# Last row of modulation sums taken from TensorE to VectorE in a diffusion-transformer layer, with one ScalarE step per inverse root and a new table of chain distances

## What is computed

```python
mod = (silu(c) @ w_mod + b_mod)              # c: 2048, w_mod: 2048 x 12288
sh1, sc1, g1, sh2, sc2, g2 = split(mod, 6)   # six rows of 2048
h  = rms_norm(x, mix_norm_pre) * (1 + sc1) + sh1
p  = h @ w_in                                # likewise for the context
o  = bidirectional chunked gated delta rule of q, k, v (8 heads, chunks of 128 tokens here)
mix = concat(rms_norm(o) * silu(z), silu(layer_norm(depthwise_conv31(glu(p)))))
x  = x + g1 * rms_norm(mix @ w_out, mix_norm_post)
hf = rms_norm(x, ffn_norm_pre) * (1 + sc2) + sh2
x  = x + g2 * rms_norm((silu(hf @ w_gate) * (hf @ w_up)) @ w_down, ffn_norm_post)
```

## Time and profile before

| | |
|---|---|
| median of 3 runs | 1611.73 us (1609.91 to 1611.95) |
| profiled execution, its own time | 1613.92 us |
| its span in the trace | 1612.2 us |
| PE busy | 1538.3 us (95%) |
| DVE busy | 1033.4 us (64%) |
| ACT busy | 739.2 us (46%) |
| POOL busy | 222.2 us (14%) |
| read from memory | 331.15 MB, 207 GB/s over the span |

### The profile page before, as it was taken

One profiled execution on the slowest core, in us unless ns is written; L12 is line 12 of the kernel. 1 busy time (PEld: TensorE's weight loads), 2 busy tenths in 40 slices (PEclk: granted clock), 3 DMA queues, 4 the chain that ended last, 5 costly groups with the idle time before them and its releaser, 6 DMA issues.

```text
span 1612.2 us, 25110 instructions
## 1 busy us (share of the span) xinstructions
PE 1538.3 (95%) x9297; PEld 1295.0 (80%) x9297; DVE 1033.4 (64%) x1435; ACT 739.2 (46%) x1042; POOL 222.2 (14%) x236
## 2 busy tenths in 40 slices
PE   3888999999999999999999999999999999999998
PEld 0557888898889888898877888888888888888786
DVE  1446899999997766665577544545454454777554
ACT  5535534443345745455357444444444443443332
POOL 2000223333242324244100000000000000000000
PEclk9998999999999999999999999999999999999999
DMA  9994566555655556564373766666666666998653
GB/s 351 382 397 116 167 199 196 190 190 183 208 179 176 171 171 209 170 196 132 118 261 117 212 194 186 192 185 192 184 193 192 187 190 191 339 321 319 222 187 136
DMA packets 190977, 334.58 MB, mean 208 GB/s; under 512 B 14706, under 2 KB 80354, under 8 KB 189985
## 3 DMA queue, kind: packets, MB, share of 16 engines
q1 hardware_dynamic: 190194, 330.89, 63.3%
q0 software_dynamic: 688, 2.39, 0.5%
HBM read 331.15 MB, written 2.10 MB: 207 GB/s over the span
## 4 chain that ended last, share of the span: by engine, by line
PE 82%; DVE 9%; DMA 2%; ACT 2%; SPq 2%; issue 2%; DVEq 0%; ACTq 0%
PE PS L1886 67%; DVE cacc L1752 3%; DMA first<-in_w_mod_dram 2%; DVE w_lo L1465 2%; PE PS L2107 2%; PE PS L2155 2%; PE PS L1892 2%; PE PS L2201 2%; SPq L756 2%; DVE sil L1586 1%; PE PS L2053 1%; PE PS L2097 1%; PE PS L1982 1%; DVE xyi L1645 1%; ACT L973 1%
## 5 line engine op out<-in xcount | busy, mean ns | idle before, releaser
L977 ACT ACTIVATE w_hi<-raw 128x1024 fp32r<-128x1024 f32 (+1 forms) x422 | 443.2, 1056 | 494.8 <-PE PS L1886 418.1
L1432 DVE TENSOR_TENSOR w_lo<-raw,w_hi 128x1024 fp32r<-128x1024 f32 x264 | 323.0, 1225 | 309.9 <-ACT w_hi L977 309.8
L1886 PE MATMUL PS<-w_hi,h_hi 128*128 128x512 f32 x704 | 275.2, 391 | 0.0
L1886 PE MATMUL PS<-w_hi,h_lo 128*128 128x512 f32 x704 | 274.3, 390 | 0.0
L1886 PE MATMUL PS<-w_lo,h_hi 128*128 128x512 f32 x704 | 274.1, 389 | 0.0
L1886 PE MATMUL PS<-h_hi,w_hi 128*128 128x256 f32 (+1 forms) x784 | 237.6, 303 | 0.0
L1465 DVE TENSOR_TENSOR w_lo<-raw,w_hi 128x1024 fp32r<-128x1024 f32 (+1 forms) x158 | 195.8, 1250 | 56.5 <-ACT w_hi L977 56.5
L1886 PE MATMUL PS<-h_hi,w_lo 128*128 128x256 f32 (+1 forms) x784 | 221.5, 283 | 0.0
L1886 PE MATMUL PS<-h_lo,w_hi 128*128 128x256 f32 (+1 forms) x784 | 221.4, 282 | 0.0
L1886 PEld LDWEIGHTS PS<-h_hi,w_hi 128*128 128x128 f32 (+1 forms) x784 | 148.3, 189 | 36.1 <-issue 32.0
L1886 PEld LDWEIGHTS PS<-w_hi,h_lo 128*128 128x128 f32 x704 | 132.3, 188 | 27.6
(11 more groups left out here) (323 smaller groups left out, 2338.4 us busy)
## 6 DMA issues: line engine op xcount, KB each, us to landing
raw<-in_w_in_dram SPq DMA_DIRECT2D x128, 512.0 KB, 3.8
raw<-in_w_mod_dram SPq DMA_DIRECT2D x96, 512.0 KB, 5.3
raw<-in_w_gate_dram SPq DMA_DIRECT2D x88, 512.0 KB, 3.6
raw<-in_w_up_dram SPq DMA_DIRECT2D x88, 512.0 KB, 3.6
raw<-in_w_down_dram SPq DMA_DIRECT2D x88, 512.0 KB, 4.6
first<-in_w_mod_dram SPq DMA_DIRECT2D x64, 512.0 KB, 9.3
raw<-in_w_out_dram SPq DMA_DIRECT2D x32, 512.0 KB, 4.3
gin<-in_w_mod_dram SPq DMA_DIRECT2D x32, 512.0 KB, 6.0
```

Of the source, the lines that this page charges most:

```text
L977: act.activation(out_ap, in_ap, ACT.Copy).then_inc(S[kind], 1)
L1432: dve.tensor_tensor(w_lo[:, slot, :], raw[:, (R0 + n) % RING, :], w_hi[:, slot, :].bitcast(F32), ALU.subtract).then_inc(S["lo"], 1)
L1886: ins = pe.matmul(out_ap, a[i], b[j], start=start and n == 0, stop=stop and n == 2, skip_group_check=grouped)
```

## The change

1. The list of groups on TensorE is cut to two (g1 and sh2), spread with the same density as before, so that they are done after two thirds of the stream. The third group, sc2, is summed on VectorE. It is cut into four quarters q of 512 columns (`NQ` = 4), each into eight steps `md (q, j)`. A step reads one ring buffer that holds two slices of 128 x 512; with the per-partition scalar silu(c) it does `mrw = raw * c` for the very first slice and `mrw = raw * c + mrw` for the others: two VectorE instructions on 512 columns a step, the second waiting for the first, and the next step waiting for this one. 32 steps, 64 instructions.
2. After the eighth step of a quarter, `mcol (2, q)` sums `mrw` over the partitions on TensorE with four matmuls, each with a block of 128 columns of `mrw` as weights and one column of ones moving, and `mcc (2, q)` adds the bias on VectorE (128 x 4). So there are four such pairs where there was one, and the ScalarE copy `mrc` of the third group is gone.
3. The steps start 4 slots (`md0`) after both the last `dw` and the second group's `mcc` are placed, and come every 6 slots (`md`). All of them are in the list before `s2`.
4. The two ScalarE steps of each inverse root become one step that issues both instructions, with a wait on a semaphore of ScalarE's own (`ch_act`) between them.
5. The table `AFTER` has new numbers. The reload of x for the FFN gets a step name of its own (`xin`) in the same place.

```diff
-AFTER = {"nr": [4, 4, 4, 7, 4, 4, 4, 2], "nr_last": [2, 17, 6, 9, 4, 5, 2, 7], ...
+AFTER = {"nr": [4, 4, 4, 7, 4, 4, 4, 0], "nr_last": [0, 19, 5, 9, 0, 9, 4, 7], ...
...
+         9], "gates": 15, "conv": 4, "rush": 1, "md": 6, "md0": 4, "vb1": [1, 2, 0, 2, 1, 3, 0, 5]}
...
-    mr = [(grp, j) for grp in range(MR) for j in range(KT)]
+    mr = [(grp, j) for grp in range(MR - 1) for j in range(KT)]
+    rows = [x for q in range(NQ) for x in [[("md", (q, j))] for j in range(KT // 2)] + [
+        [("mcol", (MR - 1, q)), ("mcc", (MR - 1, q))]]]
...
+        if row_slot[0] is None and ("dw", (NP - 1, NDW - 1)) in placed and ("mcc", (MR - 2,)) in plan:
+            row_slot[0] = slot[0] + AFTER["md0"]
+        if rows and row_slot[0] is not None and slot[0] >= row_slot[0]:
+            put(rows.pop(0))
+            row_slot[0] += AFTER["md"]
...
-            gates(MR * KT * done // total - (MR * KT - len(mr)))
+            gates((MR - 1) * KT * 3 * done // (2 * total) - ((MR - 1) * KT - len(mr)))
...
     assert not any(queue for _, queue in queues)
+    assert not rows
     plan.append(("s2", ()))
+    plan.append(("xin", ()))
...
+            if u[0] == "md":
+                _, q, j = u
+                col = (1 + MR) * D + 512 * q
+                return w_mod_v[:, 2 * j:2 * j + 2, col:col + 512]
...
+                            elif old[0] == "md":
+                                need(sp, "md", *old[1:])
...
-            def inverse_root(out_ap, log_ap):
+            n_chain = [0]
+
+            def inverse_root(out_ap, log_ap, in_ap, eps, scale):
 
                 using(EXP_LN)
+                n_chain[0] += 1
+                act.activation(log_ap, in_ap, ACT.Ln, bias=eps, scale=scale).then_inc(ch_act, 1)
+                act.wait_ge(ch_act, n_chain[0])
                 return act.activation(out_ap, log_ap, ACT.Exp, scale=-0.5)
...
                 elif kind == "s2":
-                    need(dve, "mcc", 2)
+                    need(dve, "mcc", MR - 1, NQ - 1)
...
+                elif kind == "md":
+                    q, j = key
+                    n = at_ring["md", q, j]
+                    dve.wait_ge(landed[n % RING], 16 * (n // RING + 1))
+                    if j == 0:
+                        need(dve, "mcol", *((MR - 1, q - 1) if q else (MR - 2,)))
+                    for i in range(2):
+                        part, col = raw[:, n % RING, 512 * i:512 * (i + 1)], csil[:, LAT, 2 * j + i:2 * j + i + 1]
+                        if j or i:
+                            ins = dve.scalar_tensor_tensor(out=mrw[:, :], in0=part, scalar=col, in1=mrw[:, :],
+                                                           op0=ALU.mult, op1=ALU.add)
+                        else:
+                            ins = dve.tensor_scalar(mrw[:, :], part, col, None, ALU.mult)
+                        if i == 0:
+                            step(ins)
+                    ins.then_inc(done, 1)
+                    if j < KT // 2 - 1:
+                        need(dve, "md", q, j)
...
+                elif kind == "mcol" and key[0] == MR - 1:
+                    grp, q = key
+                    need(pe, "md", q, KT // 2 - 1)
+                    b = aux(pe, kind, key)
+                    for n in range(4):
+                        ins = pe.matmul(PS[:, b, n:n + 1], mrw[:, P * n:P * (n + 1)], ones[:, 0:1], start=True, stop=True)
                     ins.then_inc(done, 1)
```

More of the change, by code:

```diff
@@ L236, in make_plan @@
     slot = [0, 0, 0]
+    row_slot = [None]
     def advance():
@@ L277, in gates @@
                 plan.append(("mrc", (grp,)))
+                if grp == MR - 2:
+                    plan.extend([("mcol", (grp,)), ("mcc", (grp,))])
         del mr[:n]
@@ L320, in make_plan @@
             gates(len(mr))
-            plan.extend([("mcol", (MR - 1,)), ("mcc", (MR - 1,))])
         rest = [c[0] for c in STREAM[n:]]
@@ L350, in make_plan @@
         unit(("wo", c, kg), QS, beside)
-    assert not late and not soon
+    assert not late and not soon and not mr
     until(("mix_lo", (NP - 1,)))
     assert not any(queue for _, queue in queues)
+    assert not rows
     plan.append(("s2", ()))
+    plan.append(("xin", ()))
     for n, (c, kg) in enumerate(WO_REST):
@@ L476, in layer @@
     SQUARED = {name: [step for step in PLAN if step[0] == name] for name in ("ysq", "psq")}
-    UNITS = [u for u in RINGED if u[0] != "mr"]
+    UNITS = [u for u in RINGED if u[0] not in ("mr", "md")]
     at_unit = {u: n for n, u in enumerate(UNITS)}
@@ L611, in sem @@
             return es.enter_context(nc.semaphore(name))
-        S = {kind: sem(f"s_{kind}") for kind in TOTALS if kind not in ("fh", "fl", "ft")}
+        S = {kind: sem(f"s_{kind}") for kind in TOTALS if kind not in ("fh", "fl", "ft", "xin")}
         S["fh"], S["fl"] = S["hi"], S["lo"]
@@ L1046, in _ @@
                     need(act, "cst")
-                    using(EXP_LN)
-                    act.activation(rtmp[:, col], sums[:, col], ACT.Ln, bias=cst[:, 0:1],
-                                   scale=1.0 / D).then_inc(S[kind], 1)
-                elif kind == "xrc":
-                    s, col = key[0], slice(2 * key[0], 2 * key[0] + 2)
-                    if s == FFN:
-                        col = slice(4 + key[1], 5 + key[1])
-                    need(act, "xrt", *key)
-                    inverse_root(rstd[:, col], rtmp[:, col]).then_inc(S[kind], 1)
-                elif kind == "nrc":
-                    need(act, "nrt", *key)
-                    a = 8 if key[1] == "k" else 12
-                    inverse_root(rstd[:, a:a + 4], rtmp[:, a:a + 4]).then_inc(S[kind], 1)
+                    inverse_root(rstd[:, col], rtmp[:, col], sums[:, col], cst[:, 0:1], 1.0 / D).then_inc(S[kind], 1)
+                elif kind == "nrc":
+                    s, what, p = key
+                    need(act, "nsq", *key)
+                    a = 8 if what == "k" else 12
+                    inverse_root(rstd[:, a:a + 4], rtmp[:, a:a + 4], sums[:, a:a + 4],
+                                 cst[:, 0:1] if what == "k" else cst[:, 1:2],
+                                 1.0 if what == "k" else float(P)).then_inc(S[kind], 1)
@@ L1066, in _ @@
+                    inverse_root(cx[:, 0, :], cx[:, 1, :], cx[:, 0, :], cst[:, 0:1], 1.0 / DC).then_inc(S[kind], 1)
                 elif kind == "yrc":
                     t, = key
-                    need(act, "yrt", t)
-                    inverse_root(rstd[:, 6 + t:7 + t], rtmp[:, 6 + t:7 + t]).then_inc(S[kind], 1)
+                    need(act, "ysm", t)
+                    inverse_root(rstd[:, 6 + t:7 + t], rtmp[:, 6 + t:7 + t], sums[:, 6 + t:7 + t], cst[:, 0:1],
+                                 1.0 / D).then_inc(S[kind], 1)
@@ L1773, in _ @@
                     dve.tensor_tensor(cacc[:, :, :], cacc[:, :, :], bc(cx[:, 0, :], 1, 8), ALU.mult).then_inc(done, 1)
+                elif kind == "md":
[16 more added lines that the diff above has]
+                        need(dve, "md", q, j)
+                elif kind == "mcc" and key[0] == MR - 1:
+                    grp, q = key
+                    need(dve, "mcol", *key)
+                    at = KT * grp + 4 * q
+                    dve.tensor_tensor(modc[:, at:at + 4], PS[:, BANK["mcol", key], 0:4],
+                                      vcol[:, VC_MR + at:VC_MR + at + 4], ALU.add).then_inc(done, 1)
                 elif kind == "mcc":
```

87 lines of the change are left out of this document (30 added, 57 removed), and 10 rows, old and new, of the table AFTER.

## The result

The changed kernel takes 1617.01 us (median of 22 runs, 1613.23 to 1620.17) where the kernel before takes 1611.74 (22 runs, 1609.63 to 1614.1): ratio 1.0032, 95% interval 1.0025 to 1.004. The forecast was 1598.3. The profiled execution of the changed kernel has 1615.24 us of its own, the one of the kernel before 1613.92: these two are 1.3 us apart and the medians 5.3, so what the traces show side by side is only a part of the loss. What the row itself costs is read further on, against a kernel without it.

The account below looks back on a forecast made before the run. Behind the taps TensorE sets the pace, with 100 us of idle VectorE beside it. -17.6 + 1.2 + 3 = -13.4 us, so 1611.73 becomes 1598.3 us; forecast 1593 to 1604 (0.60), range 1592 to 1608 (about 8 in 10).

Parts of the forecast that it names:

- What TensorE loses, 17.6 us: Sixteen modulation steps leave TensorE behind the taps, 1.10 us each: 17.6 us off (15.5 to 18.6).
- What TensorE gets, 0.6 us a column step: Four new column steps on TensorE, 2.4 us, less 1.2 for the old one: 1.2 us on (0 to 3.6).
- VectorE's 51 us: 64 new product-and-sums, 47.7 us plus 3.7 for GpSimd's interference; VectorE 81% busy from 540 to 800 us.
- The stall: TensorE waiting for VectorE in the solve, at `gh` to `z`: 3 us on (0 to 9).
- The second way: Stall estimated from TensorE's empty share against VectorE's busy share in two stretches: 1.1 points of 260 us, 2.9 us.
- the row with 0.91: Earlier trace's stretch of granted clock 0.91, where TensorE waited 2.04 us for a seed; priced 0 in the sum.
- The loads, the roots, the table: Buffers freed by VectorE (at most 2 us), joined root steps, new step distances (-4 to 2.6): 0 each.
- VectorE's queue gives half back: Rival: in-order waits on VectorE count double, leaving about -3 to -8 us: 1604 to 1609; chance 0.15.
- The solve's chain becomes the bound: Rival: from `xadd` to `z`, 21 levels each later by 1.6 us: up to +17 us, 1629; chance 0.07.
- Its point of decision: For the solve-chain rival: above a mean stall of 16.4/32 = 0.5 us a step the change loses.
- What would show it wrong: Stretch waits for `gh`, `pi`, `w_lo` over 12 us, load waits, clock below 0.97 in several slices, or unchanged output-projection start.

Follow-up runs that it names:

- no_row: Changed kernel without the third group's 32 steps, their loads and products; the four column steps kept without their wait for the products: 1600.88 us, ratio 0.9929.
- the fourth quarter alone: Changed kernel with the third group's steps, loads and waits left out for the first three quarters, only the last eight steps kept: 1601.29 us, ratio 0.9936.
- the second quarter alone: Changed kernel with only the third group's steps and loads from 610 to 685 us kept, the other three quarters left out: 1609.84 us, ratio 0.999.

## Why the prediction was wrong

- **What TensorE loses, 17.6 us.** Not measured by itself. no_row, with the steps gone and no product in their place, gains 1611.74 - 1600.88 = 10.9, where the forecast's own terms give -17.6 + 1.2 = -16.4.
- **What TensorE gets, 0.6 us a column step.** Too low by a misreading: the earlier trace rows count records, and a matmul of this form is two. "Four of them take 0.36 us" were two matmuls. A column step is eight records, 0.81 us to the next projection matmul (607.57 to 608.38) and 0.1 for that one's slower start: 4 x 0.9 - 1.2 = 2.4 us on, not 1.2. A record of one moving column takes 0.81/8 = 0.10 us, as one of 16 does. The Trainium skill (TensorEngine Tiling (Array Packing), Instruction Overhead) says that a matmul of one moving column has the latency of one with 60, and gives each an overhead of about 60 cycles. That few columns save nothing agrees with these rows; the 60 cycles, 0.025 us at 2.4 GHz by an estimate from that page's figure, do not, where the row has 0.10. Of the 5.5 us between 16.4 and 10.9 the columns are 1.2 and TensorE's waits 2.8 (8.3 for 5.5); 1.5 stay open. The two profiled executions are 13.0 us apart: 2.1 ahead of the layer norm, 13.1 from there to the output projection, and the output projection is 2.1 longer.
- **VectorE's 51 us.** Too low: the 64 products took 55.4 us, and VectorE is busy for 54.5 us more over the whole span. A product took 752 ns at the median and up to 1777, 898 in the mean of the 56 in the stretch, where the forecast had 802. That the stretch still has 211.25 us for the 211 of the forecast is luck: four products fell behind its end.
- **The stall: "I take 3 us on (0 to 9)". This is the step that failed;** measured 16.1. It was priced on one link, `gh` to `z`, with 3.7 us of slack in the mean. TensorE waits there 1.1 us in the changed kernel, 0.5 more than without the row. The row adds 8.7 us of waits, most of them elsewhere: 3.7 for the products' own column step, a wait that the change itself adds and that I had listed as 0.1 us of changeover; 2.4 for seeds and 1.2 for `xf_lat`, the longest of them directly behind products in VectorE's queue; and 1.1 through ScalarE, where `kd` holds up the copy of `pi` and `sil` the transposes. About 5.0 more come by the clock. The second way, from VectorE's share (61.5 to 81%), took a mean over stretches where the price is 0.4 us for one quarter and 9.0 for another with the same load. And no clock was in the price, though the row with 0.91 was there.
- **The loads, the roots, the table: 0 each.** Right: 0.8 us for the loads with a short product each, and ratios of 1.0002 and 1.0007 for roots and table, 1 inside both intervals. But the parts are not independent: with the products in, the old table costs 8 us.
- **The rivals.** "VectorE's queue gives half back" had the mechanism (in-order waits, the column sum, a late seed with a lower clock) at no more than 14.6 us with its columns and loads; the queue alone took 16.1. "The solve's chain becomes the bound" had the sign. Its point of decision, a mean stall of 0.51 us a step, fits by luck: 16.1/32 is 0.50, just below it, and the change loses because its gain without the row is 10.9 us and not 16.4. The way it went, every level late by a step, is not what the trace shows: the levels fall behind those of the kernel with the fourth quarter alone by 3 to 5 us at each of three places (590 to 630, 665 to 680 and 685 to 718 us) and keep step between them.
- **What would show it wrong** did: waits for `pi`, `gh` and `w_lo` stayed below the 12 us named (7.2 for `pi`, 1.1 for `gh`), but the clock was below 0.97 in three slices and the output projection started at the same time (756.6 us, before 757.6). That the FFN's length would stay the same was right.

## What to carry to other kernels

Before work is moved into an engine's gaps, look for where that engine is late without it: a stretch that is 61% busy in the mean had 13 us with a single pause of 0.7, and a quarter of the new work put there cost more than the other three. List for every step that will stand behind the new work who waits for it on each other engine, what stands behind the waiter in that queue, and who waits for the new work itself. Before a wait in the new trace is put down to the new work, look at the same place in a kernel without it: of the 2.9 us at 591 us, 2.2 were there. Price a wait of TensorE above its length, here by 0.6 to 0.8 for the clock, and look at what stands behind a wait before you take it away: with the 3.7 us for `mrw` gone, TensorE waited 4.0 for `sil`.

## What the runs showed of the hardware

- A matmul of one moving column with 128x128 weights in fp32 takes 0.20 us (four took 0.81), no less than one of 16 moving columns: six of these, twelve records, take 1.26 us in the kernel before (158.69 to 159.95).
- A product-and-sum on 32 columns takes 252 ns at the median, on 512 columns 752, on 254 columns 478: cutting the columns from 512 to 32, by 16, cut the time by three.
- Behind TensorE's wait of 3.66 us its matmuls of the solve started 0.21 us apart (678.23, 678.44, 678.65, with the second quarter alone; clock of the slice 0.87), where without the wait they started 0.11 apart (671.64, 671.75, 671.86, with the fourth alone; clock 1.00).
